# Long convolution by residues of four: 256 bins for the values and the inverse, products of sums and differences on VectorE

## The chip, the cores and the metric

One Trainium2 chip, one core of it. The time is the device time of one launch in microseconds (us). TensorE is called PE, VectorE DVE, ScalarE ACT, GpSimd POOL, SyncE SP.

## The reference

The kernel computes a two-layer block over 1024 latent tokens of width 1024 (with 256 context tokens in front). Layer 0 mixes by four heads of gated linear attention and, beside them, 512 channels of a gated long convolution; layer 1 mixes by a short convolution; each layer ends in a mixture of 32 experts. The case is about the long convolution of layer 0:

```
U = jnp.fft.rfft(uf, n=n, axis=1)                     # n = 2 * 1024, uf: 1024 x 512 channels
K = jnp.fft.rfft(h_fwd, n=n, axis=0) + jnp.conj(jnp.fft.rfft(h_bwd, n=n, axis=0))
y = jnp.fft.irfft(U * K[None], n=n, axis=1)[:, :L]
return (y + uf * skip).astype(u.dtype)
...
x0, x1, v = jnp.split(pc, 3, axis=-1)
return x0 * bidir_fftconv(v * x1, filt[0], filt[1], skip)
```

The two filters h are a small network of the position (two sine layers, then hy_w3, 64 to 1024) times a decaying window.

## The kernel before

Each engine has one instruction stream, written out in order, and waits on counting semaphores. Nothing plans it at run time. SP issues the loads in one queue. Almost all of SBUF is one arena; the names (`DFT`, `YF`, `HSUM`, ...) are views of it, many on the same words at different times, and the waits keep them apart.

The transforms are matmuls against cosine and sine tables at 512 odd frequencies (`k`, 4 chunks `kt` of 128). Time is split by parity (`par`): a spectrum at k and at 1023 - k is the sum and the difference of the even and the odd part, so only the parts are computed, each by `fn` (cosine, sine). Channels are columns (512), times or bins are partitions.

The stages around the change, in PE's order:
- The heads (`gla_head`, L1298). Behind the last head `hyena_transposes` (L1366) turns the values VX, channel-major, into VTM, time-major: for each of 4 channel groups 8 transposes of 128 columns, which read VX with a stride of 2 (L1379), and ACT copies them (L976). DVE makes the last VX by a multiply (L2023, signal `vx_ready`).
- `hyena_filters` (L1399) first runs the values' spectra of kt 0 (`spectrum`, L1388, matmul at L1395: 4 chains of 4 matmuls), then 8 chunks of 128 times of the filter projection (L1412, weights HH2, moving W3H). For each chunk ACT copies one bank (L987), DVE takes sum and difference (L2041, L2042) and windows the sum (L2046), POOL windows the difference (L702). After every second chunk PE broadcasts a gate vector (`gate_part`, L1179, matmul at L1181, which writes a bank's columns eight apart) and DVE copies it (L1895).
- `transform` (L1422): for each kt four chains for the values (kt 1 to 3) and four for the filters. ACT copies the eight banks into UK (L995). From UK the spectrum's product is formed for kt: four real rows, each four products and three sums; DVE makes rows 0 and 2 (L2055 to L2064), POOL rows 1 and 3 (L713 to L725), into YF. ACT copies the next kt only after both.
- `inverse` (L1431, matmul at L1437): for 4 channel groups and 2 parities, 2 x 4 matmuls of 512 columns from YF and IDFT; kt 0 to 2 of all groups first, kt 3 last. DVE adds the skip and multiplies by x0 (L2073, L2076).
- the output projection (L1474), whose residual add (L2088) reads x, loaded into H at L606 after the inverse.

SP's part: window table (L589), then after the last Hyena projection the hidden row HH2 (L593), W3H (L594), the 4 MB table DFT (L595, PE waits for it by `tables_in` 32, L1402); after the filters IDFT (L598); then the output weights and x. UK lies on arena words 0 to 4096, HH2 in it at 2304.

Of the kernel before, what the change touches and what calls it, by code (L numbers as in the profile page):

```python
# [21 lines left out]
P = 128  # L22
# [15 lines left out]
HW = 512  # L38
# [31 lines left out]
def constants():  # L70
# [23 lines left out]
    win = win.reshape(HALF // P, P, 2, HW).transpose(1, 2, 0, 3).reshape(P, 2 * KT * HW)  # L94

    k = np.arange(HALF)
    w = np.pi * (2 * k[None, :] + 1) * np.arange(SEQ)[:, None] / 2048.0
    cs = np.stack([np.cos(w), np.sin(w)])
    cs = cs.reshape(2, KT, P, 2, KT, P)
    fwd = cs.transpose(2, 4, 0, 3, 1, 5)  # L100
    inv = (cs / 512.0).transpose(5, 0, 3, 4, 1, 2)
# [3 lines left out]
        "idft": np.ascontiguousarray(inv.reshape(P, 8192).astype(np.float32)),  # L105
# [3 lines left out]
def build(nc, a, out):  # L109
    with ExitStack() as ctx:  # L110
# [42 lines left out]
        def bank(b):  # L153
            return ps[:, b, :]
# [175 lines left out]
        yf_dve = sem("yf_dve")  # L330
        yf_pool = sem("yf_pool")
# [126 lines left out]
        def _(sp):  # L458
# [133 lines left out]
            sp.wait_ge(flt_in, 64)  # L592
            sp.dma_start(HH2[0:HID], filter_hidden).then_inc(flt_in, 16)  # L593
# [4 lines left out]
            sp.dma_start(at(38912, 8192), a["idft"]).then_inc(tables_in, 16)  # L598
# [3 lines left out]
            sp.wait_ge(yf_dve, 2 * KT)  # L602
            sp.wait_ge(yf_pool, 2 * KT)
# [34 lines left out]
        def _(pool):  # L638
# [64 lines left out]

            base = 3
            for kt in range(KT):

                pool.wait_ge(uk_ready, 8 * (kt + 1))
                ua, ub, uc, ud, ka, kb, kc, kd = [UK[:, q] for q in range(8)]
                t0, t1 = CTMP[:, 2], CTMP[:, 3]
                for row_, terms, signs in ((1, ((ua, kb), (ub, ka), (uc, kd), (ud, kc)), (1, -1, -1)),  # L710
                                           (3, ((ua, kd), (ub, kc), (uc, kb), (ud, ka)), (1, 1, 1))):
                    base += 1
                    step(nc.gpsimd.tensor_tensor(t0, terms[0][0], terms[0][1], ALU.mult), base)  # L713
                    for q in range(3):
                        x, y = terms[q + 1]
                        base += 1
                        step(nc.gpsimd.tensor_tensor(t1, x, y, ALU.mult), base)
# [86 lines left out]
        def _(act):  # L804
# [1642 lines left out]
```

## Time and profile before

| | us |
|---|---|
| median of 3 runs | 2678.17 |
| lowest, highest | 2674.11, 2680.32 |
| the profiled execution's own time | 2692.55 |
| its span | 2690.6 |
| PE, DVE, ACT, POOL busy | 2498.0, 1026.4, 340.0, 242.9 |

The profile is of one execution; its span runs from its first instruction to its last. An engine's busy time is a mean over stages with different limits, so a stage has to be read on its own. The granted clock (PEclk) is TensorE's, in parts of full speed (2.4 GHz; the other level is 1.2 GHz). A matmul of the source on float32 is two PE instructions in the trace. PE instructions overlap, so one lasts longer than the distance to the next. "Issue to landing" is a DMA's time from its issue to its last byte.

### The profile page before, as it was taken

The page shows a single profiled execution, that of the slowest core. Times are in us where ns is not written, and L with a number is a line of the kernel's source. Part 1 is how long each engine was busy: PE and PEld are TensorE (multiplying, and loading weights), DVE is VectorE, ACT ScalarE, POOL GpSimd, SP SyncE. Part 2 cuts the span into 40 slices and gives each one's busy share as a digit, 9 for nine tenths or more (in the row PEclk, how much of TensorE's full clock was granted, in tenths as well). Part 3 has the DMA queues.
Part 4 walks back from the last instruction along what each step waited for, and adds up shares of the span by engine and source line. Part 5 has one row for each costly group of instructions (what it writes and reads, how often), then busy time and mean ns, then how long its engine had stood idle before and what let it go on. Part 6 is the DMA issues. An engine that isn't in the chain of part 4 may idle for free. (4 is left out here: it accounts for less than half of the span.)

```text
span 2690.6 us, 33060 instructions
## 1 busy us (share of the span) xinstructions
PE 2498.0 (93%) x14463; PEld 1114.3 (41%) x14464; DVE 1026.4 (38%) x1958; ACT 340.0 (13%) x664; POOL 242.9 (9%) x227
## 2 busy tenths in 40 slices
PE   5999989989999899999999799999999999999991
PEld 3455445544445533333333544444556333333330
DVE  2687477747656422222221411011464222222114
ACT  2211233321011100000000310000111000000001
POOL 2000000017600000000000000000000000000000
PEclk8999999989999899999999899999998999999995
DMA  9475001210120689999998611110006999999975
GB/s 335 173 261 196 16 24 32 77 79 10 63 86 29 255 341 388 381 392 379 371 370 348 222 39 41 30 55 31 24 32 259 355 390 392 398 398 385 382 281 216
DMA packets 121869, 574.15 MB, mean 213 GB/s; under 512 B 11743, under 2 KB 48807, under 8 KB 94712
## 3 DMA queue, kind: packets, MB, share of 16 engines
q1 hardware_dynamic: 104328, 528.56, 51.5%
q0 software_dynamic: 17312, 43.16, 4.1%
q8 instruction: 116, 1.90, 0.3%
q10 hardware_dynamic: 80, 0.26, 0.0%
q14 instruction: 33, 0.27, 0.0%
HBM read 550.71 MB, written 38.01 MB: 219 GB/s over the span
## 5 line engine op out<-in xcount | busy, mean ns | idle before, releaser
L1609 PE MATMUL ps<-arena 128*32 128x512 f32 x6144 | 689.7, 601 | 30.7 <-DMA arena<-in_ex_w_dram 30.3
L1609 PEld LDWEIGHTS ps<-arena 128*32 128x32 f32 x6144 | 199.0, 111 | 453.4 <-issue 452.2
L1633 PE MATMUL ps<-arena 128*32 128x512 f32 x3072 | 343.5, 599 | 12.2 <-DMA arena<-in_ex_w_dram 12.2
L1711 PE MATMUL ps<-arena 128*128 128x512 f32 x768 | 333.3, 596 | 4.5 <-ACT arena L1013 4.5
L2275 DVE TENSOR_SCALAR arena<-ps,gain_x,mod 128x128 f32<-128x128 f32 x384 | 126.8, 402 | 374.4 <-PE ps L1594 374.4
L1474 PE MATMUL ps<-arena 128*128 128x512 f32 x512 | 226.6, 597 | 2.9 <-DVE arena L2076 1.6
L1711 PEld LDWEIGHTS ps<-arena 128*128 128x128 f32 x768 | 146.7, 191 | 188.5 <-issue 188.5
L1633 PEld LDWEIGHTS ps<-arena 128*32 128x32 f32 x3072 | 108.0, 111 | 238.7 <-issue 238.7
L2307 DVE SCALAR_TENSOR_TENSOR arena<-ps,arena,gates 128x512 f32<-128x512 f32 x96 | 72.1, 751 | 268.1 <-PE ps L1633 268.1
L1294 PE MATMUL ps<-arena 128*128 128x512 f32 x384 | 167.3, 593 | 0.7 <-issue 0.7
L2283 DVE TENSOR_TENSOR arena<-arena,ps 128x512 f32<-128x512 f32 x48 | 52.5, 1094 | 273.5 <-PE ps L1609 273.5
L1474 PEld LDWEIGHTS ps<-arena 128*128 128x128 f32 x512 | 95.1, 190 | 113.3 <-issue 109.1
L1073 ACT ACTIVATE arena<-ps 128x512 f32<-128x512 f32 x48 | 28.7, 597 | 745.3 <-PE ps L1576 745.3
L2409 DVE TENSOR_TENSOR arena<-arena,ps 128x1024 f32<-128x1024 f32 x8 | 9.8, 1222 | 284.8 <-PE ps L1711 284.8
L1395 PE MATMUL ps<-arena 128*128 128x512 f32 x256 | 113.6, 607 | 3.8 <-DVE arena L2046 3.1
L744 POOL DMA_INDIRECT expert_rows<-arena x48 | 48.1, 1003 | 754.6 <-DVE arena L2307 754.6
L1294 PEld LDWEIGHTS ps<-arena 128*128 128x128 f32 x384 | 72.0, 190 | 88.1 <-issue 87.6
L1863 DVE SCALAR_TENSOR_TENSOR arena<-arena,silu_c 128x512 f32<-128x512 f32 x120 | 90.2, 752 | 4.3
L734 POOL DMA_INDIRECT arena<-normed_rows,arena x48 | 48.7, 1014 | 377.6 <-PE ps L1594 302.2
L1395 PEld LDWEIGHTS ps<-arena 128*128 128x128 f32 x256 | 49.7, 195 | 66.6 <-issue 61.7
L1071 ACT ACTIVATE arena<-ps 128x512 f32<-128x512 f32 x48 | 28.7, 598 | 355.1 <-PE ps L1609 355.1
L1125 PE MATMUL ps<-constants 128*128 128x256 f32 x270 | 72.1, 419 | 0.0
(276 smaller groups left out, 2193.3 us busy)
## 6 DMA issues: line engine op xcount, KB each, us to landing
arena<-in_ex_w_dram SPq DMA_DIRECT2D x192, 2048.0 KB, 11.9
arena<-in_mod_w_dram SPq DMA_DIRECT2D x24, 2048.0 KB, 8.7
arena<-expert_rows SPq DMA_DIRECT2D x16, 1024.0 KB, 8.1
arena<-in_od_w_in_dram SPq DMA_DIRECT2D x24, 512.0 KB, 6.4
arena<-in_x_dram SPq DMA_DIRECT2D x2, 4096.0 KB, 14.8
normed_rows<-arena POOLq DMA_DIRECT2D x16, 512.0 KB, 2.9
arena<-in_ev_w_in_dram SPq DMA_DIRECT2D x3, 2048.0 KB, 13.1
arena<-in_ev_w_in_dram SPq DMA_DIRECT2D x12, 512.0 KB, 4.2
```

The source lines that it names most:

```text
L734: pool.indirect_dma_start(XG[:, b], None, rows_hn, bass.IndirectOffsetOnAxis(ap=PASS_TOK[:, p:p + 1], axis=0), bounds_check=SEQ - 1, oob_i ...
L1125: nc.tensor.matmul(bank(b)[:, 0:256], ident, cst[:, 0:256], start=True, stop=True)
L1294: ins = nc.tensor.matmul(bank(6 + half), HYP[n % 3][:, j], u_part(half, j), start=j == 0, stop=j == KC - 1)
L1395: ins = nc.tensor.matmul(bank((q + 4) % 8), DFT[:, kt, fn, par, tc * P:(tc + 1) * P], rhs, start=tc == 0, stop=tc == KT - 1)
L1474: ins = nc.tensor.matmul(bank(m % 4), mixed[:, j, i * P:(i + 1) * P], slab(first[half], KC, 512)[:, j], start=j == 0, stop=j == KC - 1)
L1609: ins = nc.tensor.matmul(bank(2 + m)[c:c + n], x[:, j, c:c + n], w_slot(e % 2, m, KC, FE)[:, j], start=j == 0, stop=j == KC - 1)
L1633: ins = nc.tensor.matmul(bank(5 + half)[c:c + n], HT[:, j * P + c:j * P + c + n], w_slot(e % 2, 2, FC, D)[:, j, half * 512:(half + 1) * 51 ...
L1711: ins = nc.tensor.matmul(bank(2 * k + half), slab(L1_IN + c, 3, KC, P)[:, k, j], u_part(half, j), start=j == 0, stop=j == KC - 1)
L1863: link(V.scalar_tensor_tensor(out=acc, in0=w[:, j], scalar=silu_c[:, j, 0:1], in1=acc, op0=ALU.mult, op1=ALU.add))
L2275: ins = V.tensor_scalar(XT[:, b, j * P:(j + 1) * P], bank(j // 4)[:, (j % 4) * P:(j % 4 + 1) * P], gain_x[:, 2 * l + 1, j:j + 1], mod[:, l ...
L2283: return V.tensor_tensor(HS.rearrange("t (c p) -> t p c", p=P), SL.rearrange("t (p c) -> t p c", c=FC), bank(3).rearrange("t (p c) -> t p ...
L2307: V.scalar_tensor_tensor(out=YS[:, b, cs], in0=bank(5 + half), scalar=PASS_GATE[:, p:p + 1], in1=gates[:, 1, cs], op0=ALU.mult, op1=ALU.mu ...
```

## The change

Time is split by its residue modulo four. The values' spectra are computed at 256 bins only (chunks 0 and 2 of a reordered k: low bins, then 511 minus them); sums and differences of the residues' parts give the others. `residue` runs 16 chains of 2 matmuls for them, all ahead of the filter projection. ACT copies the second bank of each pair to USECOND, DVE writes sum and difference to USUM, which has two groups; the second lies on VTM and is written when all 16 chains have ended. The filters' spectra keep their 64 matmuls, and ACT copies only the odd part (KODD); DVE forms sum and difference in KB.

The products are formed from sums and differences of the parities: per kt 16 DVE instructions in place of 14 on DVE and 14 on POOL. POOL has no part in them. After kt 1 and kt 3, DVE folds YF of two kt (8 instructions). Before the first kt, it folds USUM (16 instructions). The inverse has 256 bins and four residues: 64 matmuls of 256 columns in place of 64 of 512, each writing every second column of its bank, in two halves (`g`). The inverse's table has 2 MB in place of 4. HH2 moves to the words of X1C (20480), and SP waits for `vx_ready` before it loads it. Transposes and filter weights are read with a stride of 4 and not 2.

```
+    win = win.reshape(2, P, 2, 2, HW).transpose(1, 3, 2, 0, 4).reshape(P, 2 * KT * HW)
+    low = np.arange(HALF // 2).reshape(2, P)
+    k = np.stack([low[0], HALF - 1 - low[0], low[1], HALF - 1 - low[1]]).reshape(HALF)
     w = np.pi * (2 * k[None, :] + 1) * np.arange(SEQ)[:, None] / 2048.0
     cs = np.stack([np.cos(w), np.sin(w)])
-    cs = cs.reshape(2, KT, P, 2, KT, P)
-    fwd = cs.transpose(2, 4, 0, 3, 1, 5)
-    inv = (cs / 512.0).transpose(5, 0, 3, 4, 1, 2)
+    fwd = cs.reshape(2, 2, P, 2, 2, KT, P).transpose(2, 5, 0, 4, 3, 1, 6)
+    inv = (cs / 1024.0).reshape(2, SEQ // 4, 4, KT, P)[:, :, :, 0::2].transpose(4, 3, 0, 2, 1)
         "dft": np.ascontiguousarray(fwd.reshape(P, 8192).astype(np.float32)),
-        "idft": np.ascontiguousarray(inv.reshape(P, 8192).astype(np.float32)),
+        "idft": np.ascontiguousarray(inv.reshape(P, 4096).astype(np.float32)),
...
-        IDFT = at(38912, 2, 2, KT * HALF)
+        IDFT = at(38912, 2, 2, SEQ)
         HSUM, HDIF = at(4096, 2 * KT, HW), at(30720, 2 * KT, HW)
-        UK = at(0, 8, HW)
+        USUM = [at(0, 8, HW), at(34816, 8, HW)]
+        PTMP = [at(20480, 2, HW), at(47104, 2, HW)]
+        USECOND = at(30720, 4, HW)
+        KB, KODD = at(43008, 2, 4, HW), at(21504, 2, HW)
+        def folds_before(kt):
+            return 32 + 4 * kt + 8 * (kt // 2)
+        def times(par, tc):
+            first = par + 2 * (tc // 2) + 4 * (tc % 2) * P
+            return slice(first, first + 4 * P - 3, 4)
+        def quarter(g, r, fn):
+            return YF[:, 2 * g + r // 2, (2 * fn + r % 2) if r < 3 else 3 - 2 * fn]
         ZT, ARG, TURNS, HH1 = at(47104, SEQ), at(46080, SEQ), at(45056, SEQ), at(44032, SEQ)
-        HH2_EARLY, HH2, W3H = at(47104, SEQ), at(2304, SEQ), at(21504, SEQ)
+        HH2_EARLY, HH2, W3H = at(47104, SEQ), at(20480, SEQ), at(21504, SEQ)
         WIN = at(43520, 2 * KT, HW)
...
             sp.wait_ge(hy_mm, 6 * HC)
             sp.wait_ge(flt_in, 64)
+            sp.wait_ge(vx_ready, HC)
             sp.dma_start(HH2[0:HID], filter_hidden).then_inc(flt_in, 16)
             sp.dma_start(W3H[0:HID], a["hy_w3"][0]).then_inc(flt_in, 16)
             sp.dma_start(at(12288, 8192), a["dft"]).then_inc(tables_in, 16)
             sp.wait_ge(filt_win, 4 * KT)
-            sp.dma_start(at(38912, 8192), a["idft"]).then_inc(tables_in, 16)
+            sp.dma_start(at(38912, 4096), a["idft"]).then_inc(tables_in, 16)
-            sp.wait_ge(yf_dve, 2 * KT)
-            sp.wait_ge(yf_pool, 2 * KT)
+            sp.wait_ge(products, KT)
             load(L0_OUT, slab(L0_OUT, KC, 512), a["ev_w_out"][0, :, 512:].rearrange("(j p) n -> p j n", p=P))
...
-            base = 3
-            for kt in range(KT):
-                pool.wait_ge(uk_ready, 8 * (kt + 1))
-                ua, ub, uc, ud, ka, kb, kc, kd = [UK[:, q] for q in range(8)]
-                t0, t1 = CTMP[:, 2], CTMP[:, 3]
...
-            for q in range(4):
-                act.wait_ge(dft_mm, q + 1)
-                nc.scalar.activation(UK[:, q], bank((q + 4) % 8), ACT.Copy).then_inc(uk_ready, 1)
+            for g in range(2):
+                for i in range(4):
+                    act.wait_ge(dft_mm, 8 * g + 2 * i + 2)
+                    if g:
+                        act.wait_ge(butterfly, 2 * (i + 1))
+                    nc.scalar.activation(USECOND[:, i], bank((2 * i + 4) % 8 + 1), ACT.Copy).then_inc(uk_ready, 1)
             for kt in range(KT):
                 if kt:
-                    act.wait_ge(yf_dve, 2 * kt)
-                    act.wait_ge(yf_pool, 2 * kt)
-                for q in range(0 if kt else 4, 8):
-                    act.wait_ge(dft_mm, 8 * kt + q + 1)
-                    nc.scalar.activation(UK[:, q], bank((q + 4) % 8), ACT.Copy).then_inc(uk_ready, 1)
+                    act.wait_ge(butterfly, folds_before(kt - 1) + 4)
+                for fn in range(2):
+                    act.wait_ge(dft_mm, 16 + 4 * kt + 2 * fn + 2)
+                    nc.scalar.activation(KODD[:, fn], bank(4 * (kt % 2) + 2 * fn + 1), ACT.Copy).then_inc(uk_ready, 1)
...
+                                                  VX[:, c, times(par, tc)], ident)
                     ins.then_inc(vx_T, 1)
             gla_projections()
@@ -1385,36 +1375,51 @@
                 gla_head(h)
             hyena_transposes(HC - 1)
-            def spectrum(kt, q):
-                fn, par = (q % 4) // 2, q % 2
-                if kt:
-                    pe.wait_ge(uk_ready, 8 * (kt - 1) + q + 1)
+            def residue(g, i, s):
+                fn, par = i % 2, i // 2
+                if g:
+                    pe.wait_ge(butterfly, 2 * (i + 1))
+                elif i == 2:
+                    pe.wait_ge(omix_ready, 2 * HEADS)
+                for tc in (2 * s, 2 * s + 1):
+                    ins = nc.tensor.matmul(bank((2 * i + 4) % 8 + s), DFT[:, 2 * g, fn, par, tc * P:(tc + 1) * P], VTM[:, par, tc],
+                                           start=tc == 2 * s, stop=tc == 2 * s + 1)
+                ins.then_inc(dft_mm, 1)
+            def filter_spectrum(kt, q):
+                fn, par = q // 2, q % 2
+                if kt >= 2:
+                    pe.wait_ge(butterfly, folds_before(kt - 2) + 4)
                 for tc in range(KT):
-                    rhs = VTM[:, par, tc] if q < 4 else (HSUM, HDIF)[fn][:, par * KT + tc]
-                    ins = nc.tensor.matmul(bank((q + 4) % 8), DFT[:, kt, fn, par, tc * P:(tc + 1) * P], rhs,
-                                           start=tc == 0, stop=tc == KT - 1)
+                    ins = nc.tensor.matmul(bank(4 * (kt % 2) + q), DFT[:, kt, fn, par, tc * P:(tc + 1) * P],
+                                           (HSUM, HDIF)[fn][:, par * KT + tc], start=tc == 0, stop=tc == KT - 1)
                 ins.then_inc(dft_mm, 1)
-                for q in range(4):
-                    spectrum(0, q)
+                for g in range(2):
+                    for i in range(4):
+                        for s in range(2):
+                            residue(g, i, s)
...
                         pe.wait_ge(filt_ready, t - 1)
+                    else:
+                        pe.wait_ge(butterfly, 14 + 2 * t)
                     for k in range(2):
...
-                    for q in range(8):
-                        if kt == 1 and q == 0:
-                            pe.wait_ge(mod_gate, 4)
-                        if kt or q >= 4:
-                            spectrum(kt, q)
+                    if kt == 1:
+                        pe.wait_ge(mod_gate, 4)
+                    for q in range(4):
+                        filter_spectrum(kt, q)
-                def part(c, par, kts, first, last):
+                def part(c, r, g):
                     for fn in range(2):
-                        for kt in kts:
-                            ins = nc.tensor.matmul(
-                                bank(2 * (c % 4) + par), YF[:, kt, 2 * fn + par, c * P:(c + 1) * P],
-                                IDFT[:, fn, par, kt * HALF:(kt + 1) * HALF],
-                                start=first and fn == 0 and kt == kts[0], stop=last and fn == 1 and kt == kts[-1])
+                        ins = nc.tensor.matmul(
+                            bank(2 * c + r % 2)[:, r // 2::2], quarter(g, r, fn)[:, c * P:(c + 1) * P],
+                            IDFT[:, g, fn, r * 256:(r + 1) * 256],
+                            start=g == 0 and r < 2 and fn == 0, stop=g == 1 and r >= 2 and fn == 1)
                     return ins
-                pe.wait_ge(yf_dve, 2 * (KT - 1))
-                pe.wait_ge(yf_pool, 2 * (KT - 1))
-                for c in range(HC):
-                    for par in range(2):
-                        q = (2 * c + par + 4) % 8
-                        pe.wait_ge(uk_ready, 8 * (KT - 1) + q + 1)
-                        part(c, par, list(range(KT - 1)), True, False)
-                pe.wait_ge(yf_dve, 2 * KT)
-                pe.wait_ge(yf_pool, 2 * KT)
-                for c in range(HC):
-                    for par in range(2):
-                        part(c, par, [KT - 1], False, True).then_inc(idft_mm, 1)
+                for g in range(2):
+                    pe.wait_ge(butterfly, folds_before(2 * g + 2))
+                    for c in range(HC):
+                        for par in range(2):
+                            if g == 0:
+                                pe.wait_ge(butterfly, folds_before(2 + c // 2) + 4)
+                            part(c, par, g)
+                            ins = part(c, par + 2, g)
+                            if g:
+                                ins.then_inc(idft_mm, 1)
...
+            for g in range(2):
+                u = USUM[g]
+                for i, (plus, minus, turned) in enumerate(((0, 4, 0), (2, 6, 1), (1, 7, 0), (3, 5, 0))):
+                    dve.wait_ge(dft_mm, 16 if g else 2 * (i + 1))
+                    dve.wait_ge(uk_ready, 4 * g + i + 1)
+                    first, second = bank((2 * i + 4) % 8), USECOND[:, i]
+                    V.tensor_tensor(u[:, plus], first, second, ALU.add).then_inc(butterfly, 1)
+                    if turned:
+                        first, second = second, first
+                    V.tensor_tensor(u[:, minus], first, second, ALU.subtract).then_inc(butterfly, 1)
...
+            for g in range(2):
+                for half in range(2):
+                    for fn in range(2):
+                        a, b = USUM[g][:, 4 * half + 2 * fn], USUM[g][:, 4 * half + 2 * fn + 1]
+                        V.tensor_tensor(a, a, b, ALU.add).then_inc(butterfly, 1)
+                        dve.wait_ge(butterfly, 16 + 8 * g + 4 * half + 2 * fn + 1)
+                        V.scalar_tensor_tensor(out=b, in0=b, scalar=-2.0, in1=a, op0=ALU.mult, op1=ALU.add)\
+                            .then_inc(butterfly, 1)
             for kt in range(KT):
-                dve.wait_ge(uk_ready, 8 * (kt + 1))
-                ua, ub, uc, ud, ka, kb, kc, kd = [UK[:, q] for q in range(8)]
-                t0, t1 = CTMP[:, 0], CTMP[:, 1]
-                for row_, terms, signs in ((0, ((ua, ka), (ub, kb), (uc, kc), (ud, kd)), (1, -1, -1)),
-                                           (2, ((ua, kc), (ub, kd), (uc, ka), (ud, kb)), (1, 1, 1))):
...
+                w = KB[:, kt % 2]
+                for fn in range(2):
+                    dve.wait_ge(uk_ready, 8 + 2 * kt + fn + 1)
+                    even = bank(4 * (kt % 2) + 2 * fn)
+                    V.tensor_tensor(w[:, 2 * fn], even, KODD[:, fn], ALU.add).then_inc(butterfly, 1)
+                    V.tensor_tensor(w[:, 2 * fn + 1], even, KODD[:, fn], ALU.subtract).then_inc(butterfly, 1)
+                dve.wait_ge(butterfly, folds_before(kt) + 4)
+                u, y = USUM[kt // 2][:, 4 * (kt % 2):4 * (kt % 2) + 4], YF[:, kt]
+                if kt:
+                    dve.wait_ge(products, kt)
+                for row, second, op in ((0, 0, ALU.subtract), (2, 2, ALU.add)):
+                    t0, t1 = (PTMP[row // 2][:, q] for q in range(2))
+                    step(V.tensor_tensor(y[:, row + 1], u[:, 0], w[:, second], ALU.mult))
+                    step(V.tensor_tensor(y[:, row], u[:, 2], w[:, 2 - second], ALU.mult))
+                    n = step(V.tensor_tensor(t0, u[:, 1], w[:, second + 1], ALU.mult))
+                    step(V.tensor_tensor(t1, u[:, 3], w[:, 3 - second], ALU.mult))
+                    settle(n)
+                    n = step(V.tensor_tensor(y[:, row + 1], y[:, row + 1], y[:, row], op))
+                    settle(n - 1)
+                    link(V.tensor_tensor(t0, t0, t1, op))
+                    step(V.tensor_tensor(y[:, row], y[:, row + 1], t0, ALU.add))
+                    ins = V.tensor_tensor(y[:, row + 1], y[:, row + 1], t0, ALU.subtract)
+                    if row:
+                        ins.then_inc(products, 1)
+                    else:
+                        step(ins)
+                if kt % 2:
+                    settle()
+                    dve.wait_ge(products, kt + 1)
+                    y, z = YF[:, kt - 1], YF[:, kt]
+                    pairs = ((y[:, 0], z[:, 0], 1), (y[:, 2], z[:, 2], -1), (y[:, 1], z[:, 3], 1), (y[:, 3], z[:, 1], 1))
+                    for p, q, sign in pairs:
+                        V.tensor_tensor(p, p, q, ALU.add if sign > 0 else ALU.subtract).then_inc(butterfly, 1)
+                    for n, (p, q, sign) in enumerate(pairs):
+                        dve.wait_ge(butterfly, folds_before(kt) + 4 + n + 1)
+                        V.scalar_tensor_tensor(out=q, in0=q, scalar=-2.0 * sign, in1=p, op0=ALU.mult, op1=ALU.add)\
+                            .then_inc(butterfly, 1)
```

## Rows read from the trace of the kernel before

**Rows 1.** The page: engines' busy time, share of the span, instructions.
```profile
PE 2498.0 (93%) x14463; PEld 1114.3 (41%) x14464; DVE 1026.4 (38%) x1958; ACT 340.0 (13%) x664; POOL 242.9 (9%) x227
```

**Rows 2.** Table by stretches: each engine's busy time (instructions), granted clock, DMA.
```profile
core 0: us, PE busy (x) PEld busy (x) DVE busy (x) ACT busy (x) POOL busy (x), PEclk, DMA share, GB/s
595.90:599.90 4.00, 4.00 (x5) 1.74 (x6) 0.55 (x1) 0.00 (x0) 0.00 (x0) 0.55 0.78 270
...
595.90:749.40 153.50, 153.33 (x352) 67.39 (x352) 98.86 (x71) 14.46 (x28) 90.01 (x56) 0.99 0.15 55
```

**Rows 3.** Waits from 540 to 752 us: who for whom, sum, times, longest.
```profile
ACT arena L995 <- POOL arena L720: 71.2, 3, 23.8
```

**Rows 4.** Timeline of PE: start, length to the last end, line; the pace of 512 columns.
```profile
552.27 15.42 PE L1395 MATMUL ps<-arena 128*128 128x512 f32 x32 [0.69 <-ACT arena L976]
567.62 3.70 PE L1412 MATMUL ps<-arena 64*128 64x512 f32 x8
...
595.90 4.63 PE L1395 MATMUL ps<-arena 128*128 128x512 f32 x6 [3.08 <-DVE arena L2046]
...
694.26 55.17 PE L1437 MATMUL ps<-arena 128*128 128x512 f32 x128 [0.17 <-ACT arena L995]
```

**Rows 5.** Groups of instructions by shape, from 540 to 770 us.
```profile
L1395 PE MATMUL ps<-arena 128*128 128x512 f32 x256 | 113.6, 607 | 3.8 <-DVE arena L2046 3.1 <-ACT arena L976 0.7
```

**Rows 6.** Timeline of SP's issues; DMA issues with size, median us to landing.
```profile
528.51 0.49 SPq L593 DMA_DIRECT2D arena<-filter_hidden  x1
...
529.69 0.58 SPq L595 DMA_DIRECT2D arena<-in_dft_dram  x1
...
arena<-in_dft_dram SPq DMA_DIRECT2D x1, 4096.0 KB, 14.6
arena<-in_ev_w_out_dram SPq DMA_DIRECT2D x2, 2048.0 KB, 8.2
```

**Rows 7.** Timeline: last multiply of the values, its transposes, the first filter chunk, the last gate copy.
```profile
548.32 1.22 DVE L2023 TENSOR_TENSOR arena<-arena 128x1024 f32<-128x1024 f32 x1
549.60 1.98 PE L1379 MATMUL ps<-constants,arena 128*128 128x128 f32 x8 [3.53 <-DVE arena L2023]
...
570.33 0.69 DVE L2041 TENSOR_TENSOR arena<-ps,arena 128x512 f32<-128x512 f32 x1 [19.46 <-issue]
570.93 0.68 DVE L2042 TENSOR_TENSOR arena<-ps,arena 128x512 f32<-128x512 f32 x1
...
595.77 0.68 DVE L1895 COPY gates<-ps 128x512 f32<-128x512 f32 x1
```

**Rows 8.** Timeline of PE: 256 columns, 128 adjacent, 64 scattered; that line's durations.
```profile
220.93 3.70 PE L1257 MATMUL ps<-arena 128*128 128x256 f32 x16
...
81.02 1.91 PE L1193 MATMUL ps<-constants,arena 128*128 128x128 f32 x16
...
571.25 2.00 PE L1181 MATMUL ps<-constants,mod 128*128 128x64 f32 x16
...
L1181 PE MATMUL ps<-constants,mod x128: 275/421/475, 571.2 to 2043.6; 128*128 128x64 f32 x128
L1257 PE MATMUL ps<-arena x160: 379/592/697, 153.6 to 224.2; 128*128 128x512 f32 x128, 128*128 128x256 f32 x32
```

**Rows 9.** Timeline of DVE: products with POOL beside them, then the inverse's copies.
```profile
612.36 0.69 DVE L2055 TENSOR_TENSOR arena<-arena 128x512 f32<-128x512 f32 x1 [15.91 <-ACT arena L995]
612.97 1.75 DVE L2058 TENSOR_TENSOR arena<-arena 128x512 f32<-128x512 f32 x1
614.75 1.64 DVE L2064 TENSOR_TENSOR arena<-arena 128x512 f32<-128x512 f32 x1
...
737.52 0.75 DVE L2073 SCALAR_TENSOR_TENSOR arena<-arena,cols,ps 128x512 f32<-128x512 f32 x1 [19.41 <-PE ps L1437]
738.30 0.69 DVE L2076 TENSOR_TENSOR arena<-arena 128x512 f32<-128x512 f32 x1
```

**Rows 10.** Timeline of DVE: the first residual, which waits for x.
```profile
762.46 0.69 DVE L2088 TENSOR_TENSOR arena<-ps,gates 128x512 f32<-128x512 f32 x1 [11.52 <-DMA arena<-in_x_dram]
```

More of the change, by code:

```diff
@@ L329, in build @@
         uk_ready = sem("uk_ready")
-        yf_dve = sem("yf_dve")
-        yf_pool = sem("yf_pool")
+        butterfly = sem("butterfly")
+        products = sem("products")
         idft_mm = sem("idft_mm")
@@ L702, in _ @@
                 nc.gpsimd.tensor_tensor(HDIF[:, t], HDIF[:, t], WIN[:, t], ALU.mult).then_inc(filt_win, 1)
-            base = 3
-            for kt in range(KT):
-                pool.wait_ge(uk_ready, 8 * (kt + 1))
-                ua, ub, uc, ud, ka, kb, kc, kd = [UK[:, q] for q in range(8)]
-                t0, t1 = CTMP[:, 2], CTMP[:, 3]
[L710 to L717, printed above, removed]
-                        dst = YF[:, kt, row_] if q == 2 else t0
-                        if q == 2:
-                            nc.gpsimd.tensor_tensor(
-                                dst, t0, t1, ALU.add if signs[q] > 0 else ALU.subtract).then_inc(yf_pool, 1)
-                            pool.wait_ge(yf_pool, 2 * kt + row_ // 2 + 1)
-                        else:
-                            base += 1
-                            step(nc.gpsimd.tensor_tensor(
-                                dst, t0, t1, ALU.add if signs[q] > 0 else ALU.subtract), base)
             def gather(l, p):
@@ L1410, in hyena_filters @@
                         pe.wait_ge(filt_ready, t - 1)
+                    else:
+                        pe.wait_ge(butterfly, 14 + 2 * t)
                     for k in range(2):
                         nc.tensor.matmul(bank(2 * (t % 2) + k),
-                                         HH2[0:HID, par + 2 * tc * P:par + 2 * (tc + 1) * P - 1:2],
+                                         HH2[0:HID, times(par, tc)],
                                          W3H[0:HID, k * HW:(k + 1) * HW], start=True, stop=True).then_inc(h3_mm, 1)
@@ L2048, in _ @@
                     gate_row(0, t // 4, t // 2 % 2)
-            for kt in range(KT):
-                dve.wait_ge(uk_ready, 8 * (kt + 1))
-                ua, ub, uc, ud, ka, kb, kc, kd = [UK[:, q] for q in range(8)]
-                t0, t1 = CTMP[:, 0], CTMP[:, 1]
-                for row_, terms, signs in ((0, ((ua, ka), (ub, kb), (uc, kc), (ud, kd)), (1, -1, -1)),
-                                           (2, ((ua, kc), (ub, kd), (uc, ka), (ud, kb)), (1, 1, 1))):
-                    step(V.tensor_tensor(t0, terms[0][0], terms[0][1], ALU.mult))
-                    for q in range(3):
-                        x, y = terms[q + 1]
-                        link(V.tensor_tensor(t1, x, y, ALU.mult))
-                        op = ALU.add if signs[q] > 0 else ALU.subtract
-                        if q == 2:
-                            V.tensor_tensor(YF[:, kt, row_], t0, t1, op).then_inc(yf_dve, 1)
-                            dve.wait_ge(yf_dve, 2 * kt + row_ // 2 + 1)
-                        else:
-                            link(V.tensor_tensor(t0, t0, t1, op))
+            for g in range(2):
[6 more added lines that the diff above has]
+                            .then_inc(butterfly, 1)
```

5 lines of the change are left out of this document (1 added, 4 removed).

## The prediction

> **What bounds the kernel now.** I read the page's busy line first, then a table by stage, the waits of the stage, and the timeline of each engine in it. On the page [rows 1] TensorE (PE) is busy for 93% of the span, VectorE (DVE) for 38%, GpSimd (POOL) for 9%. An average says little about one stage, so I cut the span at the stage's own borders [rows 2]. Between 595.9 and 749.4 us, which is the filters' spectra, the products and the inverse, PE has work in 153.3 of 153.5 us at a granted clock of 0.99, while DVE has 98.9 and POOL 90.0. So the stage ends when PE has issued its instructions. The largest wait there (ACT for POOL, 71.2 us [rows 3]) lies on engines that are ahead and costs nothing now. PE's own waits are short: 0.7 us for the transposed values at 552, 3.1 for DVE at 596 [rows 4, 5].
>
> A matmul of the source is two PE instructions, and in a full row they follow each other every 0.43 us at 512 columns: the inverse's 128 take 55.17 us [rows 4]. The spectra of values and filters are 256 instructions [rows 5]. 384 x 0.43 = 165 us: 32 instructions stand ahead of the filter chunks, 352 behind them fill the stage [rows 2, 4].
>
> **The change, part by part.** I follow the path in order of time, with the trace's clock.
>
> *The table's load (slower).* The hidden row HH2 moves onto X1C, so SP waits for vx_ready before it issues HH2, W3H and, behind them in the same queue, the 4 MB table DFT. Today SP issues the first of the three at 528.51 and the third at 529.69, and the table lands 14.6 us after its issue, at 544.3, eight microseconds before PE wants it at 552.27 [rows 4, 6]. The last vx_ready comes from the multiply that starts at 548.32 and takes 1.22 us [rows 7]: 549.55. Plus the same 1.18 us between first and third issue, plus 14.6: the table lands at 565.35. Its cover, the transposes of the last head, ends at 552.27. Cost: 13.1 us. The last head's transposes, which now read VX with stride 4 and not 2, would end before that landing even at several times their 1.98 us [rows 7]; they cost nothing while the table is late, and their own excess if it is not.
>
> *The values' spectra.* Before, 64 matmuls, of which 16 stand in front of the filters' projection and 48 in the later loop. Now 32, all in front. In front stand 64 instructions in place of 32: +32 x 0.43 = 13.8 us. The cold start is there in both (32 instructions take 15.35 us from 552.27 to 567.62 and not 13.8 [rows 4]).
>
> *The fold of the second group.* USUM[1] lies on VTM, so DVE can't write it until all 16 chains have run, and PE's next bank comes free at the 14th signal. That is 6 more DVE instructions. With one PSUM operand two in sequence start 0.60 us apart (570.33, 570.93 [rows 7]): 3.7 us, plus 0.1 for the signal. ACT's one copy of 0.6 us lies beside them. PE stands idle for it: +3.9 us. After a gap of 3.1 us the clock is seen at 0.55 for the next 4 us [rows 2, 4], which costs 1.7 us; I put 1.5 here. The bounds for this are 0 and 3.4.
>
> Through the eight filter chunks nothing changes (the same DVE, POOL and ACT work, the same two-deep ring). So the point at which the filters' spectra start, 595.90, moves by 13.1 + 13.8 + 3.9 + 1.5 = 32.3 us, to 628.2. I call it T0, and today's stage ends at T0 + 153.5.
>
> *After T0 the bound changes.* PE's work: 64 matmuls for the filters, 128 x 0.43 = 55.0 plus 1.7 cold, so at T0 + 56.7. The inverse has 64 matmuls of 256 columns. A full row of 256 columns takes 3.70 us for 16 with 0.38 for the last [rows 8]: 0.221 each, 128 x 0.221 = 28.3 us, in two halves of 14.2. By PE alone the stage would end at T0 + 85. DVE is later. Its prices: POOL has no more products, and without POOL a TENSOR_TENSOR with both operands in SBUF takes 0.69 us and the next starts 0.6 later (612.36, then 612.97 [rows 9]); with POOL beside it, it takes 1.64 to 1.75 [rows 9]. A chained pair is 0.03 longer than its first (0.75, then 0.78 to the next start [rows 9]). I take 0.60 for an unchained one, 0.72 for a chained one, 0.66 for an unchained SCALAR_TENSOR_TENSOR. From the last gate copy, which starts 0.1 before T0 (595.77 against 595.90 [rows 4, 7]) and frees DVE at T0 + 0.5:
> - folding USUM: 8 x (0.72 + 0.66) = 11.0, to 11.5.
> - the filters' sums for kt 0: the second pair waits for PE (1.7 + 13.8 = 15.5) and ACT's copy (0.8 with signals), to 17.4.
> - products of one kt: two rows of 7 x 0.60 + 0.73 = 4.93, so 9.9: to 27.3. Four sums of kt 1, the last two waiting for PE at 30.0: 31.2; products to 41.1.
> - fold of two kt: 4 x 0.60 + 4 x 0.66 = 5.1: to 46.2.
> - kt 2 and 3: PE is ahead now, so 2 x (2.4 + 9.9) + 5.1 = 29.7: to 75.9, and 76.2 with waits on its own signals.
>
> PE does the first half of the inverse from 56.7 to 70.9, stands for 5.4 us, and does the second from 76.3: 14.2, a cold start of 1.7 and 0.2 for the last: T0 + 92.4. Between its groups of eight, 1.8 us apart, DVE's pair of 1.4 to 1.5 us fits as today. So T0 + 153.5 becomes T0 + 92.4: -61.1 us. Bounds of DVE's chain: its 96 instructions with both operands in SBUF (16 + 64 + 16) take 61 us as priced; all chained at 0.75 they take 72, 11 us more, and all at 0.60, with PE's clock held, 5 us less.
>
> *What follows* is rigid. The load of x is issued at the inverse's end (L606) and holds the first residual for 11.5 us [rows 10]; it does so from the new end too. The projections' weights are released at T0 + 57 and T0 + 71 and land in 8 us, before T0 + 92. The inverse's table is half as large.
>
> **The sum.** 32.3 - 61.1 = -28.8 us. The profiled execution took 2692.55 us over a span of 2690.6, 14.4 above the median of the runs, 2678.17. It becomes 2663.8; taken off the median: 2649.4 us.
>
> **The rivals.**
>
> *The inverse's scattered columns.* Each 256-column matmul writes every other column of its bank. No row shows that shape. The nearest is the gate's broadcast, which writes 64 columns eight apart: 16 in 2.00 us with 0.28 for the last, 0.115 each, where 128 adjacent columns take 16 in 1.91 [rows 8]. From below the price is thus nothing. From above, 0.115 for 64 columns is 0.46 for 256, against 0.221. At 0.46 the inverse runs from T0 + 56.7 through 59 us with no stall to T0 + 115.8, 23.4 later: 2672.8 us. I take nothing, since the row sits on the floor that a weight load sets. The Trainium skill, "SBUF — State Buffer", in its section on Door 1, the DMA port swizzle, says that PSUM has 8-byte lines and that "any non-contiguous PSUM access pattern significantly slows down matmuls"; it gives no figure. By that rule this rival is the forecast, and the gate's row only bounds it. I give it 0.12.
>
> *The table's wait is covered.* If PE did not wait for the table (a landing in 2 us in place of 14.6), T0 would be 13 us earlier: 2636 us. Against it stands that nothing else is on the queues in today's landing either. 0.03.
>
> *The slow products stay slow (the other side).* If the 1.64 us [rows 9] came from something other than POOL, such as PE's streaming, all 96 SBUF instructions of the chain behind T0 would start 1.67 apart: folds of 26.7, products of 26.7 per kt, so that DVE ends near T0 + 170, the stage near T0 + 186, 94 later: 2743 us. It decides from the point at which the 96 lose 28.8 us, that is at 0.3 us more for each, a start every 0.93 us. Against it: the first of each burst, before POOL's first has begun, takes 0.69, and so does L2076 with PE at full stream [rows 9]. 0.03.
>
> *The pieces on the early side grow.* The clock stays low through the filter chunks, or T0's terms meet each other; that is a few microseconds, inside the range. Cases that I have not seen get 0.04.
>
> **How the numbers follow.** My own case has 0.78, with 2641 to 2657 for itself. The scattered columns at some intermediate price reach from there to 2672; I close the range at 2666, which leaves out the worst of them and the two small cases. Faster by over 0.2% (5.4 us, about what can be told here) is my case, the covered table and nearly all of the scattered columns: 0.91. Within (the gate's bound, or DVE half slow): 0.04. Slower (slow products, unseen cases): 0.05.
>
> **What would show it.** A wait of PE for the table of about 13 us at 552, the first filter chunk at some 598, a wait of about 4 before it; TENSOR_TENSOR at 0.69 in the products; the first half of the inverse done before DVE's last fold, a PE wait of 5 to 6 us for DVE between its halves; 0.22 between 256-column matmuls. Wrong it would be by a pace over 0.3 there, by DVE instructions over 0.8, or by a table that lands early.

## The result

| | before | changed |
|---|---|---|
| median of 5 runs, us | 2678.17 | 2659.40 |
| lowest, highest | 2671.59, 2680.32 | 2654.60, 2666.26 |
| the profiled execution | 2692.55 | 2666.26 |
| its span | 2690.6 | 2664.3 |

The ratio is 0.9927, 95% interval 0.9909 to 0.9945: 19.6 us less (14.7 to 24.4). The medians themselves are 18.8 us apart, and 28.8 were forecast. 2659.4 lies inside the stated range, and the direction is right, but a third of the expected gain is missing.

The profile after says where. First the page's busy line, which answers to [rows 1]:

```profile
PE 2459.2 (92%) x14399; PEld 1109.7 (42%) x14400; DVE 1018.8 (38%) x2030; ACT 332.4 (12%) x648; POOL 152.8 (6%) x171
```

POOL has lost its 90 us of products, and DVE has 72 instructions more and yet less busy time. A "cold start" in this text is work that begins while the granted clock is still at its lower level, 1.2 GHz, and waits for it to rise to 2.4. Then PE's timeline through the stage (start, length to the last end, line, idle before and its releaser), which answers to [rows 4] and [rows 7]:

```profile
547.08 1.98 PE L1369 MATMUL ps<-constants,arena 128*128 128x128 f32 x8 [3.54 <-DVE arena L2022]
564.00 30.53 PE L1386 MATMUL ps<-arena 128*128 128x512 f32 x64 [14.93 <-DMA arena<-in_dft_dram]
598.38 7.18 PE L1417 MATMUL ps<-arena 64*128 64x512 f32 x8 [3.86 <-DVE arena L2043]
605.50 3.67 PE L1171 MATMUL ps<-constants,mod 128*128 128x64 f32 x16
609.10 7.21 PE L1417 MATMUL ps<-arena 64*128 64x512 f32 x8
...
637.74 3.67 PE L1171 MATMUL ps<-constants,mod 128*128 128x64 f32 x16
641.70 56.71 PE L1396 MATMUL ps<-arena 128*128 128x512 f32 x128 [0.29 <-DVE arena L2056]
698.25 13.98 PE L1440 MATMUL ps<-arena 128*128 128x256 f32 x64
717.79 16.78 PE L1440 MATMUL ps<-arena 128*128 128x256 f32 x64 [5.56 <-DVE arena L2103]
736.13 20.87 PE L1473 MATMUL ps<-arena 128*128 128x512 f32 x48 [1.57 <-DVE arena L2116]
```

Each forecast wait is there: 14.9 us for the table, 3.9 for the fold, 5.6 between the inverse's halves. New is the length of the filter chunks, L1417 with L1171: 8 instructions take 7.2 us in place of 3.7 (L1412 in [rows 4]), and the broadcast's 16 take 3.67 in place of 2.00 [rows 8]. The table by stretches names the reason (columns as in [rows 2]); first the changed kernel, its chunks and the wait ahead of them:

```profile
564.00:594.52 30.52, 30.52 (x64) 13.16 (x64) 5.15 (x8) 4.18 (x7) 0.00 (x0) 0.91 0.00 1
594.52:598.38 3.86, 0.00 (x1) 0.03 (x1) 3.82 (x7) 0.60 (x1) 0.00 (x0) 0.82 0.00 0
598.38:641.70 43.32, 43.03 (x96) 24.09 (x96) 26.19 (x30) 4.78 (x8) 10.60 (x8) 0.50 0.00 0
641.70:645.70 4.00, 4.00 (x6) 1.89 (x7) 3.90 (x7) 0.00 (x0) 0.00 (x0) 0.62 0.80 246
645.70:712.00 66.30, 66.30 (x187) 35.24 (x185) 60.56 (x98) 4.78 (x8) 0.00 (x0) 1.00 0.13 49
```

and the chunks of the kernel before:

```profile
567.62:595.90 28.28, 24.26 (x97) 14.71 (x96) 24.51 (x28) 5.37 (x9) 10.62 (x8) 0.88 0.00 1
```

The same instructions, at a granted clock of 0.50 (1.2 GHz) from the first to the last, with PE busy for 43.03 of 43.32 us. Before, with a mean clock of 0.88, DVE with POOL paced the chunks and PE had idle time; at 0.50 PE paces them itself.

| step, in order | forecast, us | measured, us |
|---|---|---|
| PE waits for the table | +13.1 | +14.2 (14.93 - 0.69) |
| 32 more instructions of values | +13.8 | +15.2 (30.52 - 15.35) |
| fold of the second group | +3.9 | +3.9 |
| clock in the filter chunks | +1.5 | +15.0 (43.32 - 28.28) |
| from the filters' spectra to the inverse's end | -61.1 | -60.7 (92.9 for 153.5) |
| sum | -28.8 | -12.4 |

From the last head's transposes to the output projection the stage is 201.40 us before (549.60 to 751.00) and 189.05 after (547.08 to 736.13). The spans differ by 26.3 us. The rest, 2.5 us ahead of the stage and 11.4 behind it, is in code that the change doesn't touch. Behind the stage, the profiled executions of this study scatter from 1922.6 to 1939.6 us (before had the 1939.6), so a difference of 10 us between two spans proves nothing, and each experiment is read in this stretch of the trace as well as in the medians. The stage accounts for 12.4 us of the ratio's 19.6 (14.7 at the least); what makes up the rest stays open.

### The profile page after: what moved, and what is told of

The parts are those of the page before. It is cut to its first block and busy times, and to the rows that moved or that the text cites. A ratio compares the mean times of both kernels' runs of the same rounds, so it can differ in the third digit from the quotient of the medians.

```text
span 2664.3 us, 32938 instructions
## 1 busy us (share of the span) xinstructions
PE 2459.2 (92%) x14399; PEld 1109.7 (42%) x14400; DVE 1018.8 (38%) x2030; ACT 332.4 (12%) x648; POOL 152.8 (6%) x171
## 5 line engine op out<-in xcount | busy, mean ns | idle before, releaser
L1710 PE MATMUL ps<-arena 128*128 128x512 f32 x768 | 330.4, 593 | 4.5 <-ACT arena L1003 4.5
L1473 PE MATMUL ps<-arena 128*128 128x512 f32 x512 | 226.6, 597 | 2.9 <-DVE arena L2116 1.6
L1710 PEld LDWEIGHTS ps<-arena 128*128 128x128 f32 x768 | 146.0, 190 | 186.3 <-issue 186.3
L1284 PE MATMUL ps<-arena 128*128 128x512 f32 x384 | 167.3, 594 | 0.7 <-issue 0.7
L1473 PEld LDWEIGHTS ps<-arena 128*128 128x128 f32 x512 | 95.3, 191 | 112.6 <-issue 108.8
L1284 PEld LDWEIGHTS ps<-arena 128*128 128x128 f32 x384 | 72.2, 191 | 87.9 <-issue 87.4
L1208 PE MATMUL ps<-arena 128*128 128x512 f32 x160 | 70.1, 595 | 0.0
L1247 PE MATMUL ps<-arena 128*128 128x512 f32 (+1 forms) x160 | 63.3, 553 | 0.0
```

What stands on the lines that cost most here:

```text
L1208: ins = nc.tensor.matmul(bank((2, 3, 6)[i % 3]), u_cols(i, j), w[:, j], start=j == 0, stop=j == KC - 1)
L1247: ins = nc.tensor.matmul(bank(s % 4)[:, 0:n], wqk[:, j, c0:c0 + P], u_part(part, j), start=j == 0, stop=j == KC - 1)
L1284: ins = nc.tensor.matmul(bank(6 + half), HYP[n % 3][:, j], u_part(half, j), start=j == 0, stop=j == KC - 1)
L1473: ins = nc.tensor.matmul(bank(m % 4), mixed[:, j, i * P:(i + 1) * P], slab(first[half], KC, 512)[:, j], start=j == 0, stop=j == KC - 1)
L1710: ins = nc.tensor.matmul(bank(2 * k + half), slab(L1_IN + c, 3, KC, P)[:, k, j], u_part(half, j), start=j == 0, stop=j == KC - 1)
```

## The experiments

All ratios are to the kernel before, run beside each group of experiments: its median was 2679.85 us beside e1 to e4, 2678.91 beside e5 and e6, 2683.99 beside e7 and e8. So ratios compare better across the rows than medians do. The length of a traced stretch is from one execution each. "Chunks" is the time from the first filter chunk to the first filters' spectrum. "Stretch" is the time from the start of the last head's transposes to the start of the output projection, in the profiled execution.

| run | median, us | ratio (95%) | chunks, us | stretch, us |
|---|---|---|---|---|
| before | 2678.17 | 1 | 28.3 | 201.4 |
| changed | 2659.40 | 0.9927 (0.9909 to 0.9945) | 43.3 | 189.1 |
| e1_warm | 2645.46 | 0.9857 (0.9829 to 0.9885) | 28.4 | 171.7 |
| e2_table_first | 2650.76 | 0.9887 (0.9864 to 0.9910) | 43.0 | 173.1 |
| e3_both | 2631.13 | 0.9820 (0.9796 to 0.9844) | 28.4 | 158.4 |
| e4_before_gap | 2704.35 | 1.0089 (1.0067 to 1.0112) | 42.6 | 220.6 |
| e5_window_dve | 2631.61 | 0.9806 (0.9783 to 0.9829) | 25.8 | 156.0 |
| e6_before_all_dve | 2682.67 | 1.0002 (0.9986 to 1.0018) | 28.3 | 201.2 |
| e7_warm_twice | 2633.07 | 0.9812 (0.9798 to 0.9825) | 25.7 | 154.8 |
| e8_warm_late | 2657.19 | 0.9901 (0.9885 to 0.9916) | 36.8 | 179.9 |

**e1_warm: fill the wait ahead of the chunks.**

```
                             residue(g, i, s)
+                pe.wait_ge(uk_ready, 5)
+                spare(8, 5)
                 pe.wait_ge(flt_in, 96)
```

Two lines ahead of the filter chunks: 8 matmuls of 256 columns into a bank that is free by then. `spare(n, bank)` is a helper that the kernel already has; it multiplies constants by the identity, and nobody reads what it writes.

> The changed kernel, with 8 spare 256-column matmuls (16 PE instructions, some 3.5 us) behind the values' spectra, in the 3.9 us in which PE waits for DVE's fold. Theory A (the clock that PE carries into the filter chunks decides the clock in them): in the changed kernel's trace the chunks run at the lower clock from 598.4 to 641.7, 43.3 us, against 28.3 us in the kernel before. With the wait filled, they start at the full clock and the first six take some 22 us as before, so the stretch from the last values' spectrum to the first filter spectrum shrinks from 47.2 us to 32 to 34 us and the median falls by 13 to 15 us, to about 2645 us. Rival B (the chunks' own load, 64-row matmuls and 64-column broadcasts with waits between, sets the clock whatever came before): the stretch stays within 2 us of 47.2 and the median within 2 us of the changed kernel's.

PE's timeline:

```profile
564.23 29.72 PE L1386 MATMUL ps<-arena 128*128 128x512 f32 x64 [12.97 <-DMA arena<-in_dft_dram]
593.78 3.62 PE L1115 MATMUL ps<-constants 128*128 128x256 f32 x16
597.81 3.79 PE L1419 MATMUL ps<-arena 64*128 64x512 f32 x8 [0.41 <-DVE arena L2045]
601.53 2.00 PE L1171 MATMUL ps<-constants,mod 128*128 128x64 f32 x16
...
626.19 56.95 PE L1396 MATMUL ps<-arena 128*128 128x512 f32 x128 [2.86 <-DVE arena L2058]
```

The chunks are back at 28.4 us, from 43.3, with 3.6 us of work that computes nothing in a wait that PE had anyway. From the last values' spectrum to the first filter spectrum it is now 32.4 us. Theory A holds; B is out. It is 13.9 us faster than the changed kernel by the medians and 18.7 by the ratios, with 10 to 28 possible by the intervals of both. The runs scatter more than those of the changed kernel, from 2630.5 to 2650.3 us, and why stays open. Of the 17.4 us that the stretch lost, 2.0 are the table, which landed sooner in this execution (a wait of 12.97 for 14.93).

**e2_table_first: undo the late load.**

```
             sp.wait_ge(hy_mm, 6 * HC)
+            sp.dma_start(at(12288, 8192), a["dft"]).then_inc(tables_in, 16)
             sp.wait_ge(flt_in, 64)
             sp.wait_ge(vx_ready, HC)
...
-            sp.dma_start(at(12288, 8192), a["dft"]).then_inc(tables_in, 16)
```

> The changed kernel, with the load of the 4 MB table issued ahead of the wait for vx_ready, and only HH2 and W3H behind it. Theory A: PE's 14.9 us wait for the table before the values' spectra goes to under 1 us and nothing else needs it, so the median falls by about 14 us, to about 2645 us; the clock in the filter chunks stays low, since the 3.9 us wait ahead of them remains. Rival B: the wait for the table is what cools PE for the chunks too; then they run at full clock and the gain is near 28 us, to about 2631. Rival C: another wait takes the table's place (HH2 and W3H land late, the transposes with stride 4 are slow) and the gain is under 8 us.

```profile
553.23 29.15 PE L1386 MATMUL ps<-arena 128*128 128x512 f32 x64 [0.69 <-ACT arena L965]
586.25 6.82 PE L1417 MATMUL ps<-arena 64*128 64x512 f32 x8 [3.86 <-DVE arena L2043]
593.00 3.67 PE L1171 MATMUL ps<-constants,mod 128*128 128x64 f32 x16
```

PE's wait for the table is gone (0.69 us, as before the change), no other wait took its place, and the stretch is 15.9 us shorter. The last transposes, which now read with a stride of 4, took 1.98 us as they did with a stride of 2, so rival C's slow transposes are out too. The chunks stay slow, 43.0 us: the 14.9 us wait is not what takes their clock; e1 and e4 show that the 3.9 us wait is. That is A against B. The median fell by 8.6 us only, by the ratios 10.7, where 14 were forecast; with the intervals of both some 3 to 18 is possible. The medians alone thus can't tell A from C, and the trace does.

**e3_both: both edits.** The two diffs together.

> Both edits: the table's load first, and the 8 spare matmuls. If the two costs are separate, the gains add: 14 + 14, about 2631 us. If filling the wait does nothing for the clock, about 2645 us as with the table alone.

2631.13 us: 28.3 under the changed kernel, 30.7 in the stretch. The two costs are separate and add up: 15.9 us for the table and 14.9 for the chunks make 30.8. With its two side effects undone, the change is worth 1.8% and not 0.7%.

**e4_before_gap: the wait alone, in the kernel before.**

```
+            dve.wait_ge(dft_mm, 4)
+            for _ in range(5):
+                link(V.tensor_tensor(CTMP[:, 0], VX[:, 0, 0:HW], VX[:, 0, HW:], ALU.add))
+            dve.sem_inc(gap, 1)
             dve.wait_ge(tables_in, 32)
...
                 pe.wait_ge(flt_in, 96)
+                pe.wait_ge(gap, 1)
```

> The kernel before, with one wait of about 3.9 us added for PE ahead of the filter chunks: DVE does five chained 512-column additions into a scratch area behind the fourth values' chain, and PE waits for them. Theory A (a wait of this length drops the clock and the chunks then never win it back): the chunks take 40 to 43 us in place of 28.3, and the time rises by 3.9 plus 12 to 15 us, 16 to 19 us in all, to about 2695 us. Rival B (the chunks' low clock in the changed kernel has another cause, such as the wait for the table 30 us earlier): the time rises by the wait and a cold start, 4 to 6 us, to about 2683 us.

```profile
552.59 15.39 PE L1396 MATMUL ps<-arena 128*128 128x512 f32 x32 [0.69 <-ACT arena L977]
571.77 6.48 PE L1414 MATMUL ps<-arena 64*128 64x512 f32 x8 [3.79 <-issue]
578.18 3.67 PE L1182 MATMUL ps<-constants,mod 128*128 128x64 f32 x16
...
614.33 46.12 PE L1396 MATMUL ps<-arena 128*128 128x512 f32 x100 [0.29 <-DVE arena L2052]
```

and its chunks in the table by stretches:

```profile
571.77:614.33 42.56, 42.27 (x97) 23.59 (x97) 25.14 (x28) 4.78 (x8) 10.60 (x8) 0.51 0.00 1
```

One wait of 3.79 us in an otherwise unchanged kernel costs 19.2 us in the stretch (3.8 of it the wait, 14.3 the chunks) and 24 by the ratio (18 to 30). The forecast was 16 to 19 us in all. With e1 this shows the cause from both sides: with the wait the chunks are slow, and without it, or with work in its place, they are not. What was not tried is how short such a wait may be.

**e5_window_dve: no POOL in the chunks either.** In e3's kernel:

```
-                nc.gpsimd.tensor_tensor(HDIF[:, t], HDIF[:, t], WIN[:, t], ALU.mult).then_inc(filt_win, 1)
+                V.tensor_tensor(HDIF[:, t], HDIF[:, t], WIN[:, t], ALU.mult).then_inc(filt_win, 1)
```

> The version with the table first and the spare matmuls (2631 us), and in it the windowing of the differences moved from POOL to DVE too. There seven of DVE's eight windowings of the sums took 1.75 us beside POOL's in place of 0.69. Theory A (POOL's reads of SBUF are what stretches a DVE instruction with two SBUF operands): all 16 windowings take 0.69 on DVE, a chunk costs DVE 0.6 x 4 and a chain gap, some 2.6 us in place of 3.1 to 3.3, so the chunks end 3 to 5 us earlier (23 to 26 us from 583.95 in place of 28.4) and the median is about 2627 us. Rival B (the stretch comes from PE's or ACT's traffic at that place, POOL or not): DVE gets eight more instructions of 1.7 us, the chunks take 10 us longer, about 2642 us.

DVE's timeline in it, a sum's and a difference's window behind each other:

```profile
592.83 0.69 DVE L2054 TENSOR_TENSOR arena<-arena 128x512 f32<-128x512 f32 x1
593.44 0.68 DVE L2055 TENSOR_TENSOR arena<-arena 128x512 f32<-128x512 f32 x1
```

Moving POOL's work onto the busier engine made each of that engine's windowings shorter: all 16 take 0.68 or 0.69 us, where seven of e3's eight took 1.75 or 1.76. The chunks take 25.8 us, inside the 23 to 26 forecast for their length, but that is 2.6 fewer where 3 to 5 were forecast. The stretch is 2.4 us shorter, and the medians (2631.61 against 2631.13) and the ratios (0.9806 and 0.9820) can't tell so little.

**e6_before_all_dve: one part of the change alone.** The kernel before, with POOL's two rows of products put behind DVE's, same form, POOL's loop deleted.

> The kernel before, with one part of the change alone: all products on DVE, none on POOL, the transform as it was. Theory A: without POOL a chained TENSOR_TENSOR there takes 0.69 to 0.73 us in place of 1.64; the 28 of one kt take some 20.5 us on DVE, where 14 beside POOL's 14 took 23.3. PE bounds that stage (27.5 us for one kt), so the time stays the same within 3 us. Rival B (the stretch is not POOL's doing): 28 x 1.67 = 47 us for one kt against PE's 27.5, four times, some 75 us slower.

Two of the products' groups in it (count, busy us, mean ns):

```profile
L2047 DVE TENSOR_TENSOR arena<-arena 128x512 f32<-128x512 f32 x24 | 16.5, 690 | 0.5
L2034 DVE TENSOR_TENSOR arena<-arena 128x512 f32<-128x512 f32 x24 | 16.5, 690 | 0.5
```

28 products and sums take 19.8 us (611.61 to 631.41) on DVE alone. Side by side, DVE's 14 took 22.4 us and POOL's 14 ended 23.5 us after the first began (612.36 to 635.91 in the kernel before). The time is the same, ratio 1.0002, since PE bounds that stage. So "all on VectorE" gives nothing by itself in the old transform. In the new one DVE is the bound; what it would take there with POOL still at work was not run.

**e7_warm_twice: the second cold start too.** In e5's kernel, 6 spare matmuls ahead of `pe.wait_ge(filt_win, 4 * KT)`.

> The version with the table first, the spare matmuls and all windowing on DVE, and 6 more spare matmuls (2.6 us) in the 3.0 us in which PE waits for the last windowing. There the filters' spectra began at 0.5 to 0.6 of the clock and took 57.9 us for 128 instructions, against 55.2 at the full clock. Theory A (PE is what DVE waits for in the first chunk of the spectra, so the cold start is on the path): the spectra take 55.2 to 55.5 us and the stretch from the last transposes to the output projection, 156.0 us there, shrinks by 2 to 2.7 us; the median falls by as much, to some 2629 us, which the spread of the runs hides. Rival B (DVE's chain alone sets the end): PE gains the 2.7 us and the stretch stays within 0.5 us.

```profile
608.77 2.81 PE L1111 MATMUL ps<-constants 128*128 128x256 f32 x12
611.92 55.20 PE L1392 MATMUL ps<-arena 128*128 128x512 f32 x128 [0.35 <-DVE arena L2057]
666.96 13.98 PE L1440 MATMUL ps<-arena 128*128 128x256 f32 x64
686.50 17.14 PE L1440 MATMUL ps<-arena 128*128 128x256 f32 x64 [5.57 <-DVE arena L2104]
```

The spectra take 55.20 us, and the second half of the inverse starts 74.6 us behind their start, where it was 77.3 in e5: the 2.7 us were on the path. But that half then takes 17.14 us, 15.70 in e5, which gives 1.4 back. In the other kernels of this study it took 15.7 to 16.9 behind the same wait, so the length of that cold start varies and the 1.4 can't be laid to the edit. The stretch is 1.1 us shorter, between A and B. In the medians it can't be told.

**e8_warm_late: the same spare work, inside the chunks.** In the changed kernel, `spare(8, 7)` behind the first gate broadcast.

> The changed kernel with the 3.9 us wait left as it is, and the 8 spare matmuls put behind the first gate broadcast, inside the filter chunks. Theory A (the low clock lasts because the chunks' instructions don't bring it back, and a dense run of full matmuls does): 16 instructions take some 6 us, the clock rises during them, and the chunks behind run at the full clock; the chunks take 11 + 6 + 20, some 37 to 39 us in place of 43.3, so 4 to 6 us are won back. Rival B (nothing inside the chunks brings the clock back before their end): the spares cost their 7 us at the lower clock, and the chunks take 50 us.

```profile
604.74 3.67 PE L1171 MATMUL ps<-constants,mod 128*128 128x64 f32 x16
608.21 4.77 PE L1115 MATMUL ps<-constants 128*128 128x256 f32 x16
612.91 3.82 PE L1417 MATMUL ps<-arena 64*128 64x512 f32 x8
616.66 2.00 PE L1171 MATMUL ps<-constants,mod 128*128 128x64 f32 x16
```

The clock comes back within the spares (0.77 over their 4.77 us, 1.00 behind them), and the next group takes 3.82 and 2.00 us. Theory A holds. The chunks take 36.8 us, a little under the 37 to 39 forecast: 6.6 won, where the same 8 matmuls ahead of them win 14.9. Which property of the chunks' instructions keeps the clock from coming back by itself, the 64 rows, the 64 columns or the mixture, was not tried.

## Why the prediction was right in its sign and short by a third

*The bound after the change* was right. With POOL silent, DVE's instructions take what one row had shown [rows 9]:

```profile
661.62 0.68 DVE L2085 TENSOR_TENSOR arena<-arena 128x512 f32<-128x512 f32 x1
662.22 0.68 DVE L2087 TENSOR_TENSOR arena<-arena 128x512 f32<-128x512 f32 x1
662.94 0.69 DVE L2088 TENSOR_TENSOR arena<-arena 128x512 f32<-128x512 f32 x1
```

0.60 between unchained ones, 0.72 behind a chained one. T0, the start of the filters' spectra, is 641.70 here. DVE's chain ended its last fold at T0 + 76.0 (forecast 76.2), the stage at T0 + 92.9 (92.4).

*The table's load* was right in kind: 14.2 us for 13.1. It landed in 15.6 us, not 14.6, in this execution; e1's took 13.6.

*The values' spectra* were 1.4 us short: "the cold start is there in both" took the two starts as alike, but PE came to the one out of 0.7 us of idling and to the other out of 14.9, and the first 4 us behind that are at 0.50, where the other's are at 0.64.

*The failed step* is "Through the eight filter chunks nothing changes", together with the 1.5 us for the clock, whose bounds were "0 and 3.4". The bounds came from a row in which a dense run of 512-column matmuls follows a short wait and the clock is back some 4 us later [rows 2, 4]. Behind the new wait come other instructions, 64 rows deep or 64 columns wide, and under them it was not back after 43 us (changed, e2, e4). The term measured 15.0 us. The text had the case in one sentence ("the clock stays low through the filter chunks") and priced it at "a few microseconds" without doing the sum: 96 instructions of the chunks at half the clock are PE's 24.3 busy microseconds grown to 43, beyond DVE's pace.

The trace of the kernel before held a warning. The row was read as "after a gap of 3.1 us the clock is seen at 0.55", but the clock had been lost before that gap, inside the chunks:

```profile
587.29 1.99 PE L1412 MATMUL ps<-arena 64*128 64x512 f32 x4 [0.94 <-DVEq L2045]
589.21 3.62 PE L1181 MATMUL ps<-constants,mod 128*128 128x64 f32 x16
```

The granted clock is 1.00 up to 589.2 and 0.51 in the 3.62 us of the last broadcast, which the three broadcasts ahead of it did in 2.00. PE had stood still for only 0.94 us, 2 us earlier. The same happens in e1, e3 and e6, and in e8 behind its spares, each time behind a wait of 0.57 to 0.95 us inside the chunks. e5 and e7 have no such wait, and their chunks run at the full clock to the end. That the short wait is the cause there was not tested by itself, but the row showed that these instructions can lose the clock and do not win it back at once.

*Luck in the range.* The case that was argued had 2641 to 2657 for itself, and 2659.4 lies outside it. It is in the stated range only because that was widened to 2666 for scattered columns, which cost nothing. In the stage the terms missed by 16.4 us (1.1 the table, 1.4 the spectra, 13.5 the clock, 0.4 the rest), and the median by 10.0; the stage's 12.4 us alone would have put it at 2665.8. The other 6.4 us came in the forecast's favour and are the part that stays open above.

*The rivals.* Scattered columns: out. 64 matmul instructions that write every second column of a bank took 13.98 us, 0.38 of it the last: (13.98 - 0.38) / 63 is 0.216 us each, against 0.221 for adjacent columns [rows 8]. The rule of the Trainium skill ("SBUF — State Buffer", section on Door 1) that a non-contiguous PSUM pattern slows matmuls significantly does not hold for this shape: the trace disagrees, and it decides. Slow products: out in the changed kernel, and e5 and e6 show the other half: with POOL's instructions beside them they take 1.63 to 1.76 us (before, e3), with those gone 0.69. Covered table: out, by the row of its wait.

## What to carry to other kernels

A wait that a change adds for TensorE must be priced with what runs behind it. Ahead of a dense run of full matmuls this kernel paid 1.5 to 3.1 us for the clock (56.7 to 57.9 us for the filters' spectra against 55.2, 15.7 to 17.1 for the inverse's second half against 13.98), ahead of light ones 15 us. A few spare matmuls in such a wait are cheap, and ahead of the light stretch they are worth twice what they are inside it. When a buffer moves onto another, look at everything queued behind the load that must now wait; here a 256 KB load held up a 4 MB one, and issuing the large one first gave 16 us of the stretch back. The best version measured, e3 with or without e5's edit, is at 2631 us, 1.8 to 1.9% under the kernel before. And work shared out to GpSimd can cost VectorE more than it takes off it: 14 and 14 side by side held VectorE for 22.4 us, 28 alone for 19.8.

## What the runs showed of the hardware that I had not expected

- TensorE stayed at 1.2 GHz for 43 us while it was busy for 99% of them, with 64-row and 64-column matmuls, and was back at 2.4 GHz within 4.8 us of 256-column ones (e8). The same light instructions entered at 2.4 GHz kept it for 22.7 us, to their end, where PE never stood still among them (e5), and lost it within about 2 us of a wait of 0.65 to 0.95 us where they had one (before, e1, e3, e6).
- Matmuls of 256 columns into every second column of a PSUM bank are as fast as into adjacent ones (0.216 and 0.221 us).
- A VectorE instruction with both operands in SBUF took 0.69 us with GpSimd silent (changed, e6) and 1.63 to 1.76 us beside a GpSimd one (before, e3).
